# Two attentions of a transformer block: outputs by feature, probabilities divided before the transposes

## The reference

```
logits = einsum('bqhd,bshd->bhqs', qb, k) * (QK_DIM ** -0.5)   # sa: one k for all heads, + bias
p = softmax(where(mask, logits, NEG), axis=-1)
out = einsum('bhqs,bshd->bqhd', p, v)                          # 64 features of a head
h = h + out.reshape(b, s, 1024) @ w_o
```

## Time and profile before

| | |
|---|---|
| median of 3 runs | 1713.39 us (1711.52 to 1713.49) |
| span of the profiled execution | 1711.1 us |
| TensorE busy | 1397.3 us (82%) |
| VectorE, ScalarE, GpSimd busy | 536.3, 389.7, 132.3 us |
| chain that ended last | PE 47%, DMA 47%, DVE 3% |

### The profile page before, as it was taken

One profiled execution on the slowest core, in us unless ns is written; L12 is line 12 of the kernel. 1 busy time (PEld: TensorE's weight loads), 2 busy tenths in 40 slices (PEclk: granted clock), 3 DMA queues, 4 the chain that ended last, 5 costly groups with the idle time before them and its releaser, 6 DMA issues.

```text
span 1711.1 us, 21197 instructions
## 1 busy us (share of the span) xinstructions
PE 1397.3 (82%) x8724; PEld 855.2 (50%) x8724; DVE 536.3 (31%) x899; ACT 389.7 (23%) x579; POOL 132.3 (8%) x108
## 2 busy tenths in 40 slices
PE   4999997676666667757766766898999999999999
PEld 2986542222122112212221221476899998989997
DVE  2785310000000000000000000058365557835554
ACT  3515200000000000000000000057443346843332
POOL 1430000000000000000000000004500000730000
PEclk8999988877878877787877787899999999999999
DMA  9777599999999999999999999992154544425552
GB/s 376 263 290 301 228 382 426 429 427 429 429 429 429 429 428 429 429 428 428 428 429 428 428 429 429 428 344 99 52 195 179 178 162 149 143 99 197 195 179 93
DMA packets 80325, 542.05 MB, mean 317 GB/s; under 512 B 6312, under 2 KB 9721, under 8 KB 52626
## 3 DMA queue, kind: packets, MB, share of 16 engines
q1 hardware_dynamic: 76912, 535.93, 76.8%
q0 software_dynamic: 1632, 5.03, 1.0%
q10 hardware_dynamic: 1730, 0.36, 0.1%
HBM read 540.22 MB, written 1.08 MB: 316 GB/s over the span
## 4 chain that ended last, share of the span: by engine, by line
PE 47%; DMA 47%; DVE 3%; ACT 1%; issue 1%; POOL 1%; SPq 0%; DVEq 0%; ACTq 0%; POOLq 0%
DMA ring<-in_w_down 22%; DMA ring<-in_w_up 21%; PE bank L1387 10%; PE bank L1389 10%; PE bank L1388 10%; PE bank L1754 4%; PE bank L1773 3%; PE bank L1640 2%; DMA ring<-in_a_w_in 2%; DMA ring<-in_w_mod 1%; DMA ring<-in_w_in 1%; PE bank L1423 1%; PE bank L1621 1%; PE bank L1561 1%; PE bank L1733 1%
## 5 line engine op out<-in xcount | busy, mean ns | idle before, releaser
L1754 PE MATMUL bank<-ring,low 128*32 128x512 f32 x2016 | 314.5, 769 | 152.1 <-DMA ring<-in_w_up 125.7
L1754 PEld LDWEIGHTS bank<-ring,low 128*32 128x32 f32 x2016 | 66.6, 130 | 381.0 <-DMA ring<-in_w_up 192.5
L1773 PE MATMUL bank<-ring,low 128*32 128x512 f32 x976 | 167.7, 822 | 93.7 <-DMA ring<-in_w_down 86.6
L1133 ACT ACTIVATE low<-bank 128x512 f32<-128x512 f32 x16 | 9.6, 597 | 844.8 <-PE bank L1754 844.8
L927 ACT ACTIVATE ring_parts<-ring 128x4096 fp32r<-128x4096 f32 (+3 forms) x46 | 151.9, 3301 | 205.8 <-DMA ring<-in_mlp_w_down 101.0
L2083 DVE TENSOR_TENSOR ring_parts<-ring,ring_parts 128x4096 fp32r<-128x4096 f32 (+2 forms) x35 | 148.5, 4244 | 141.0 <-ACT ring_parts L927 141.0
L1388 PE MATMUL bank<-feat_parts,ring_parts 128*128 128x256 f32 x640 | 181.6, 284 | 0.0
L1389 PE MATMUL bank<-feat_parts,ring_parts 128*128 128x256 f32 x640 | 181.6, 284 | 0.0
L1387 PE MATMUL bank<-feat_parts,ring_parts 128*128 128x256 f32 x608 | 173.4, 285 | 6.8 <-DVE feat_parts L2153 3.7
L2429 DVE TENSOR_TENSOR low<-low,bank 128x512 f32<-128x512 f32 x16 | 11.0, 688 | 462.4 <-PE bank L1754 462.4
L1773 PEld LDWEIGHTS bank<-ring,low 128*32 128x32 f32 x976 | 31.7, 131 | 210.2 <-DMA ring<-in_w_down 135.3
(11 more groups left out here) (407 smaller groups left out, 1979.9 us busy)
## 6 DMA issues: line engine op xcount, KB each, us to landing
ring<-in_w_gate SPq DMA_DIRECT2D x64, 2048.0 KB, 25.7
ring<-in_w_up SPq DMA_DIRECT2D x62, 2048.0 KB, 23.0
ring<-in_w_down SPq DMA_DIRECT2D x61, 2048.0 KB, 26.2
ring<-in_mlp_w_up SPq DMA_DIRECT2D x16, 2048.0 KB, 7.8
ring<-in_mlp_w_down SPq DMA_DIRECT2D x16, 2048.0 KB, 7.9
ring<-in_w_mod SPq DMA_DIRECT2D x11, 2048.0 KB, 15.5
ring<-in_w_in SPq DMA_DIRECT2D x3, 2048.0 KB, 13.3
ring<-in_a_w_in SPq DMA_DIRECT2D x3, 2048.0 KB, 16.1
```

Source lines behind the costliest of these rows:

```text
L1754: last = pe.matmul((GATE if i < 4 else UP)[32 * j:32 * j + 32, :], xsT[:, k, :], held(n, 2)[:, kk, 512 * j:512 * j + 512], start=(k == 0), ...
L1773: last = pe.matmul(TURN[32 * g:32 * g + 32, :], hidT[:, c, 32 * j:32 * j + 32], down_row(n, c, d), start=(j == 0 and c < 2), stop=(j == 3 ...
```

## The change

It does the division before the transposes. Each head's probabilities are multiplied in SBUF, in place, by the reciprocal of their sum, a scalar per partition (`scaled`), and the transposes of a head wait for that (semaphore `_scaled`). The outputs have the values stationary, 64 columns for each head; the first head goes to the left half of the array's columns and to partitions 0 to 63 of the bank, the second to the right half, and the 128 columns of `pT` move. The result is by feature at once, so O banks, the division on the way out (L2290) and the turns (L1600) go. In sa the tokens come out reversed, and the copies of the parts read them through a reversed view (`pair_out`). In sa the bias and the maximum of a head become one `tensor_tensor_reduce`, which leaves the negated sum and its minimum, and the exponentials have scale -1. The banks have new homes, and rounded and low parts come one step earlier.

```diff
@@ TensorE
+                def outputs(i):
+                    out, nb = bk(f"{pre}X{i // 2}")[:, P * (i % 2):P * (i % 2 + 1)], tile_step(i)[0] + 1
+                    pe.wait_ge(*drained(f"{pre}T{i}"))
+                    if i % 2 == 0:
+                        banks.wait_free(pe, f"{pre}X{i // 2}")
+                    for b in range(nb):
+                        for h in range(2):
+                            last = pe.matmul(out[HD * h:HD * (h + 1), :], values(i, h, b), pT[i % 4][:, h * nb + b, :],
+                                             start=(b == 0), stop=(b == nb - 1), skip_group_check=True)
+                    if i % 2:
+                        end(last, f"{pre}X{i // 2}")
...
-                        pe.wait_ge(*drained(f"{pre}S{i}"))
                         banks.wait_free(pe, f"{pre}T{i}")
                         for b in range(2 * n // P):
+                            if b % (n // P) == 0:
+                                pe.wait_ge(sem(pre + "_scaled"), 2 * i + b // (n // P) + 1)
                             last = pe.transpose(...)
...
-                    if 0 < i <= N_AT:
-                        pe.wait_ge(*drained(f"{pre}T{i - 1}"))
-                        banks.wait_free(pe, f"{pre}O{i - 1}")
-                        nb = tile_step(i - 1)[0] + 1
-                        for h in range(2):
-                            for b in range(nb):
-                                last = pe.matmul(bk(f"{pre}O{i - 1}")[:, HD * h:HD * (h + 1)], pT[(i - 1) % 4][:, h * nb + b, :],
-                                                 outputs(i - 1, h, b), start=(b == 0), stop=(b == nb - 1))
-                        end(last, f"{pre}O{i - 1}")
-                    if i >= 3 and i % 2:
-                        turn_out((i - 3) // 2)
+                    if i:
+                        outputs(i - 1)
@@ VectorE
-                def output(i):
+                def scaled(i):
+                    n = tile_step(i)[1]
                     dve.wait_ge(*drained(f"{pre}S{i}"))
                     link(dve.reciprocal(at_r[:, i % 4, :], at_s[:, i % 4, :]))
-                    dve.wait_ge(*banks.filled(f"{pre}O{i}"))
-                    first = HD * head_at(i, 0)
-                    dve.tensor_tensor(split(token_out[:, i // 8, first:first + 2 * HD], 2), split(bk(f"{pre}O{i}")[:, 0:2 * HD], 2),
-                                      at_r[:, i % 4, :].unsqueeze(2).to_broadcast([P, 2, HD]), ALU.mult)                        .then_inc(banks.drain_sem(f"{pre}O{i}"), 1)
+                    for h in range(2):
+                        p = pexp[i % 3][:, n * h:n * (h + 1)]
+                        dve.tensor_scalar(p, p, at_r[:, i % 4, h:h + 1], None, ALU.mult).then_inc(sem(pre + "_scaled"), 1)
...
                     if i + 2 < N_AT:
                         maxima(i + 2)
-                    if i:
-                        output(i - 1)
-                    if i >= 4 and i % 2 == 0:
-                        low_out((i - 4) // 2)
-                    if between:
-                        between(i)
+                    if i + 1 < N_AT:
+                        scaled(i + 1)
+                    if i >= 3 and i % 2:
+                        low_out((i - 3) // 2)
+                    between(i)
...
-                link(dve.tensor_tensor(s, s, strips[:, pair_heads(i), P * (1 - t):P * (1 - t) + n], ALU.add))
+                for h in range(2):
+                    s = bk(f"saS{i}")[:, n * h:n * (h + 1)]
+                    last = dve.tensor_tensor_reduce(s, s, strips[:, head_at(i, h), P * (1 - t):P * (1 - t) + n], -1.0, -NEG,
+                                                    ALU.add, ALU.min, at_m[:, i % 4, h:h + 1])
```

More of the change, by code:

```diff
@@ L528, in two_blocks, with pair_groups, fill, scores @@
         group("q2T0", "q2T1", among=unscored)
[L530 to L538, removed]
+        def pair_groups(pre, beside):
+            first = (banks.last + 1) % 8
+            def fill(name, home):
+                group(name, among=[(first + home) % 8])
+            def scores(i):
+                fill(f"{pre}S{i}", i if i < 3 else (4, 2)[i - 3] if i < 5 else (4, 0, 1, 2)[(i - 5) % 4])
+            for i in range(2):
+                scores(i)
+            for i in range(N_AT + 1):
                 if i + 2 < N_AT:
-                    fill(f"{pre}S{i + 2}")
+                    scores(i + 2)
                 if i < N_AT:
-                    fill(f"{pre}T{i}")
-                if 0 < i <= N_AT:
-                    fill(f"{pre}O{i - 1}")
-                if i >= 3 and i % 2:
-                    fill(f"{pre}X{(i - 3) // 2}")
-                fill(*beside.get(i, ()))
+                    fill(f"{pre}T{i}", 3 if i == 0 or i >= 4 and i % 2 == 0 else 5)
+                if i % 2:
+                    fill(f"{pre}X{i // 2}", 6 + i // 2 % 2)
+                for name, home in beside.get(i, ()):
+                    fill(name, home)
         LATE_QUERIES = 0
-        pair_groups("sa", {LATE_QUERIES: ("q2T2", "q2T3")})
+        pair_groups("sa", {LATE_QUERIES: (("q2T2", 6), ("q2T3", 7))})
         out_groups("ao", wo2)
@@ L579, in query_turn @@
             eng.tensor_tensor(qr, qr, rot, ALU.add).then_inc(sem("q3"), 1)
-        steps = ((1, "O0", 0), (1, "q4", 6), (1, "q5", 7), (1, "q6", 1), (1, "q7", 3), (2, "S4", 2), (2, "T2", 5), (2, "O1", 0),
[3 rows of a table removed]
-        home = {("q3T" if g[0] == "q" else "la" + g[0]) + g[1:]: b for _, g, b in steps}
-        pair_groups("la", {LATE_TURN: [f"q3T{i}" for i in range(4, 8)]}, home)
+        pair_groups("la", {LATE_TURN: tuple(zip((f"q3T{i}" for i in range(4, 8)), (7, 0, 1, 3)))})
         out_groups("bo", wo3)
@@ L1322, in la_scale @@
                 return qs[2][:, n:n + 1]
-            attend_pairs("la", boT, None, la_scale, la_beside)
+            attend_pairs("la", boT, la_scale, beside=la_beside)
             weights_high(first_mlp[1])
@@ L1585, in attend_local, with attend_pairs @@
                         local_turn(j - 2)
-            def attend_pairs(pre, scores, outputs, token_out, order, between=None):
+            def attend_pairs(pre, scores, values, between):
                 def score_group(i):
@@ L1591, in score_group @@
                     scores(i)
[L1593 to L1599, removed]
-                        last = pe.transpose(bk(f"{pre}X{j}")[:, a * P:(a + 1) * P], token_out[:, t, k * P:(k + 1) * P], order)
-                    end(last, f"{pre}X{j}")
+                def outputs(i):
[7 more added lines that the diff above has]
+                                             start=(b == 0), stop=(b == nb - 1), skip_group_check=True)
+                    if i % 2:
+                        end(last, f"{pre}X{i // 2}")
                 score_group(0)
                 score_group(1)
-                for i in range(N_AT + 2):
+                for i in range(N_AT + 1):
                     if i + 2 < N_AT:
```

65 lines of the change are left out of this document (27 added, 38 removed), and 3 rows, old and new, of the table steps.

## The result

The changed kernel takes **1731.9 us** (median of 4 runs, 1730.1 to 1734.3) beside 1713.1 for the kernel before (4 runs, 1711.5 to 1713.5): ratio 1.011, 95% interval 1.010 to 1.0125. Its profiled execution took 1731.5 us with a span of 1729.7, 18.6 more than before's 1711.1. The forecast was 1731.

A forecast was written before the change was run, and what follows sets the result against it. It took weights from memory to bound the experts and TensorE block two; sa +7 and la +11 gave +18 on the span of 1711.1, and the 2.3 between median and span was carried over: 1731 us, range 1712 to 1739.

The forecast's parts named there:

- The mechanism: Both attentions: VectorE's multiplications wait for the GpSimd instruction in flight, and TensorE's transposes wait for them; +18 us in sum.
- The second multiplication waits for a whole further GpSimd instruction: Each step's pair beside GpSimd: the second also waits, so sa steps take 2.6 or 3.9 us, taken as 3.05.
- Rival 3: Both attentions: half the waits, the second multiplication goes right through; +8, 1721 us; chance 0.12.
- sa, +7 forecast: Sparse attention: waits put step 11's transposes +7.9 us later, later steps and tail give -1.1; together +7 us.
- under 0.3 after it: Sign in the multiplication's rows: 0.3 to 1.5 us while GpSimd works, under 0.3 us after it.
- the way out, -1.1: End of sa: the four steps left save 0.7 us, the tail 0.8 less 0.4 for the last multiplications.
- Switching the array: TensorE's outputs in column halves: switching included, 0.77 us a long step and 0.55 a short one.
- the 0.33 for a trip: TensorE's outputs: entering column halves costs 0.14 us and leaving 0.19, read from the expert products.
- la, +11 forecast: Latent attention: waits put step 9's transposes +12.5 us later, remaining steps and tail give back 1.6; +11 us.
- rival 4: Both attentions: TensorE's clock falls as well, to half for some 16 steps; +24 on top, 1754 us; chance 0.05.
- rival 1: Both attentions: multiplications don't wait and switching the array costs nothing; faster, about 1708 us; chance 0.10.
- rival 2: Both attentions: no waits, switching at 0.33; sa -1.4, la +0.8, no change at 1713 us; chance 0.10.

The follow-up runs named there:

- a: The changed kernel with GpSimd's output-weight splits delayed until the last maximum of each attention: 1750.1 us.
- c: The changed kernel with the reciprocal in PSUM and one multiplication for both heads, steps 2 and 3 in the old form: 1718.5 us.
- d: The changed kernel with GpSimd's splits in instructions half as wide and twice as many: 1724.6 us.
- k: The changed kernel with three filler products of the identity ahead of the transposes of steps 0 to 7: 1728.8 us.
- f: The changed kernel without the multiplications, probabilities left undivided, so not the reference's result: 1709.9 us.
- j: The changed kernel with the outputs of step i-1 ahead of the transposes of step i: 1730.3 us.
- i: Kernel c with the outputs of step i-1 ahead of the transposes of step i: 1716.0 us.

## Why the prediction was right

**The mechanism** is shown. The waits end where GpSimd's instruction ends. Two of the product L2752 in la, and GpSimd then:

```profile
1496.48 1.21 DVE L2752 TENSOR_TENSOR st<-st 128x2 f32<-128x2 f32 x1
...
1502.64 0.87 DVE L2752 TENSOR_TENSOR st<-st 128x2 f32<-128x2 f32 x1
```

```profile
1496.40 1.27 POOL L835 TENSOR_TENSOR ring_parts<-ring,ring_parts 128x512 fp32r<-128x512 f32 x1
...
1502.23 1.27 POOL L835 TENSOR_TENSOR ring_parts<-ring,ring_parts 128x512 fp32r<-128x512 f32 x1
```

They end at 1497.69 and 1503.51, GpSimd at 1497.67 and 1503.50. The multiplications of sa's step 10 and GpSimd beside the second of them:

```profile
1207.79 0.44 DVE L2273 TENSOR_SCALAR brow<-brow,st 128x256 f32<-128x256 f32 x1
...
1208.15 1.36 DVE L2273 TENSOR_SCALAR brow<-brow,st 128x256 f32<-128x256 f32 x1
```

```profile
1208.04 1.32 POOL L804 TENSOR_TENSOR ring_parts<-ring,ring_parts 128x512 fp32r<-128x512 f32 x1
```

The second ends at 1209.51 and GpSimd at 1209.36. Of the fourteen multiplications in steps 5 to 11 of sa, thirteen end 0.08 to 0.16 us behind an instruction of GpSimd; the last began as GpSimd stopped and took 0.34 us. a up to step 13 (no GpSimd), c (no second SBUF input) and d (shorter instructions) each take the waits away or shorten them.

**"The second multiplication waits for a whole further GpSimd instruction"** holds nearly throughout. The pairs of sa's steps 5 to 11 took 2.08, 1.88, 2.52, 1.74, 2.61, 1.72 and 1.60 us, where 0.48 (to step 7) and 0.62 are undisturbed. In the first six the second of the pair took 1.30 to 1.36 us, a whole instruction, every time; only the last, when GpSimd stopped, had 0.34. What varied was the first, 0.44 to 1.34, by where in GpSimd's instruction it came. In la the second waited out a whole instruction in eight pairs of ten, but mostly a cast (0.63) and not a subtraction (1.29 to 1.43). Rival 3, in which it goes right through, has 2 of 16 pairs for it.

**sa, +7 forecast, +5.6 measured.** Counted from the first scores, step 11's transposes came 1212.16 - 1178.89 = 33.3 us in, against 25.6 before: +7.7, where +7.9 was forecast; the seven steps took 20.3 us, 2.90 each, where I had put 3.05. The misses are inside: GpSimd was not held up as I had reckoned (its instructions took 1278 ns in the median beside 1285 before, and it ended at 1211.9, not 1213), the fused operation takes 0.72 for both heads, not 0.80, and an undisturbed multiplication of 256 elements 0.35, not 0.29, so that my sign "under 0.3 after it" failed. The term that was too small is the way out, -1.1: from there to the product it is 9.4 us against 11.5, so -2.1. Two steps of 2.33 instead of 2.51 give 0.4 of it, and 1.7 come behind step 13, where the last turn with its wait and the dearer outputs are gone.

**Switching the array** was priced well: the long step is 2.31, from 2.48 by the parts in the forecast (the text rounded these to 2.4; two such steps of the trace before, 1205.16 to 1210.18, are 5.02). But outputs take 0.58 and not the 0.7 to 0.8 that I had named as the sign: of the 0.33 for a trip only 0.15 stands in the outputs. The rest is in their neighbours: 0.09 in the transposes, now 0.53 from start to start instead of 0.44, and 0.06 to 0.1 in the scores behind the outputs, now 1.20 instead of 1.10 to 1.14.

**la, +11 forecast, +13.3 measured**, and it was right for reasons that were partly others. Step 9's transposes came +13.5 late (1505.10 - 1474.44 = 30.7 against 17.2), near the +12.5 forecast. But the seven short steps took 21.0 us where I had 18.9 (the late q turns alone took 3.56 us instead of 1.91, at the lower clock), and the two long ones 6.5 where I had 7.8, and these not by two pairs of GpSimd: from 1500 TensorE never waited, and its half clock made the next steps 3.5 and 4.0 us long. This is the mechanism of rival 4, "the clock falls as well", to which I gave 0.05 and then only for whole attentions. It came true as a part: 3.3 us by k, not 24. Its argument, 3.26 busy of 5 us at a clock of 0.66, was better than "the gaps here are about 1 us", with which I dismissed it. The early steps of la had gaps of 1.52, 0.81 and 0.98 us. Behind step 9 the forecast -1.6 came out as -0.2, the slow step included. With the clock held at 1.00 (k) la lost 9.9 us, fillers included, so my waits alone, at +11, were put too high and the clock at nothing. The two errors have opposite signs, and that the sum came within 1 us of the measured 1731.9 is luck.

**Rivals 1 and 2**, in which the multiplications don't wait, have an answer too. f, which has no multiplications at all, took 1709.9; c, whose multiplications hardly wait, took 1718.5, where rival 1 had 1708 and rival 2 1713. Both had put the longer way to the transposes at nothing, as my own sum did. The step from 2.51 to 2.31 is a gain of 0.20, where rival 1 had 0.51 and the experts' rows gave 0.18: measurement decides for the rows. Beside rival 1 stood the Trainium skill, page "TensorEngine Tiling (Array Packing)", section "Theoretical Speedup", which gives up to 2x for column halves. The trace stays below that: 0.58 us for outputs that I had estimated at 0.88 one after the other.

**Not forecast:** that a multiplication almost without waits would still cost 8.5 us over none (c against f).

## What to carry to other kernels

Before work is put on VectorE beside a GpSimd that reads and writes SBUF, look at what the shortest VectorE instruction with all its inputs in SBUF takes there: if two elements take half a microsecond, as in the earlier trace rows, each such instruction added costs up to a whole GpSimd instruction, and the second of two in a row nearly always does; its undisturbed length says nothing. Of 18.8 us an input in PSUM bought back 13.4 here, and GpSimd instructions of half the length 7.3. A step put between two engines' hand-overs can cost time even where both engines have room (8.5 us from f to c), until other work is moved into the gap; and gaps of about a microsecond may cost TensorE's clock on top, as in la of the change.

## What the runs showed that I had not expected

**The clock fell at the first gaps of an attention** in most kernels with the multiplication, with or without GpSimd: 0.83 in 1190 to 1200 in c and in a, and in the changed kernel 0.79 in 1191.9 to 1200 with full speed behind it. In la of the change it read 0.67 over the 35 us from the first scores, in j, with the outputs first, it read 0.66 in 1480 to 1490 and 1.00 behind. Why it came back early in one and late in the other was not settled; three fillers a step kept it at 1.00. In i and f it read 1.00 throughout sa. In la of f, which has no multiplication, it still read 0.83 in 1470 to 1480, with gaps of 0.79 and 0.57 us before it, so the multiplication is not needed for a fall there.

**GpSimd hardly pays.** I took from the earlier trace rows that each would hold up the other. In sa its sixteen instructions took 20.00 us instead of 19.75, while single multiplications beside them took up to 1.36 us (up to 1.43 in la).
